# FoX heads half a head behind the GDN heads, two weight slots and a gather ring of six in a hybrid decoder step

## What is computed

```python
qkv_g, a_g, b_g, z_g, qkv_f, f_f, og_f = split_in(rmsnorm(hp, norm_mix[l]) @ w_in[l])
# GDN, 8 heads of 128: short causal conv + SiLU on q|k|v, gated delta rule in chunks,
#   output = rmsnorm_head(o) * silu(z)
# FoX, 8 heads of 128: softmax attention with query/key norm and forget gates,
#   output = rmsnorm_head(o) * sigmoid(og)
hp = hp + merge_heads(o_gdn, z_g, o_fox, og_f, ...)          # concat @ w_out
hp = hp + peer(rmsnorm(hp, norm_ffn[l]), w_query, sub_keys, expert_u, expert_v)
```

## Time and profile before

| what | us |
|---|---|
| median of three runs | 4675.52 |
| the profiled execution, its own time | 4657.51 |
| its span | 4655.7 |
| group a: norm; heads; output, norm and routing | 0 to 54; 54 to 907; 917 to 1212 |
| group b: norm; heads | 1212 to 1293; 1293 to 2414 |
| group b: output projection; norm; routing | 2427 to 2600; 2600 to 2655; 2655 to 2985 |
| rest of the experts | 2985 to 4656 |

### The profile page before, as it was taken

The page is one execution under the profiler, slowest core; times in us unless marked ns, Lnnn a source line. Parts: engine busy times, 40 slices in busy tenths (PEclk is TensorE's granted clock), DMA queues, the critical chain, the costliest instruction groups (busy, mean ns, idle before and its releaser), DMA issues. The chain is left out here.

```text
span 4655.7 us, 35143 instructions
## 1 busy us (share of the span) xinstructions
PE 2418.1 (52%) x11713; PEld 1909.2 (41%) x11713; DVE 3374.0 (72%) x4421; ACT 545.6 (12%) x1307; POOL 2361.1 (51%) x1217
## 2 busy tenths in 40 slices
PE   6999999898488888888759564200000000000000
PEld 5888888677466656666547443100000000000000
DVE  1333333307749989989877588799898989989998
ACT  1222222200122212222210010000000000000000
POOL 1110001000226676656565322288888888888886
PEclk8999999799699999999859777655555555555555
DMA  6666666386759999999999855499999999999998
GB/s 188 210 189 203 210 203 192 112 291 228 265 209 402 410 391 393 395 391 395 339 363 408 309 203 203 154 416 422 404 419 405 411 413 420 420 412 422 411 417 355
DMA packets 443932, 1513.69 MB, mean 325 GB/s; under 512 B 42044, under 2 KB 276208, under 8 KB 277848
## 3 DMA queue, kind: packets, MB, share of 16 engines
q0 software_dynamic: 161840, 1158.85, 61.7%
q1 hardware_dynamic: 269240, 251.94, 17.0%
q10 hardware_dynamic: 12672, 100.67, 5.4%
HBM read 1384.96 MB, written 126.21 MB: 325 GB/s over the span
## 5 line engine op out<-in xcount | busy, mean ns | idle before, releaser
L1929 DVE SCALAR_TENSOR_TENSOR ex_y<-ex_ring,ex_wt,ex_y 128x2048 f32<-128x2048 f32 x538 | 1264.4, 2350 | 122.5 <-DMA ex_ring<-in_peer_v_dram,idx_all 74.4
L1914 DVE CUSTOM_DVE_ANT_0 ex_ring<-ex_ring,ex_xi 128x2048 f32<-128x2048 f32 x544 | 1244.7, 2290 | 141.2 <-DMA ex_ring<-in_peer_u_dram,idx_all 50.5
L1836 POOL DMA_INDIRECT ex_ring<-in_peer_u_dram,idx_all x384 | 794.4, 2069 | 341.2 <-DVE ex_hid L1914 136.3
L1836 POOL DMA_INDIRECT ex_ring<-in_peer_v_dram,idx_all x384 | 823.5, 2145 | 221.7 <-DVE ex_hid L1914 115.9
L1868 PE MATMUL ex_fold<-ex_y,const 128*32 128x512 f32 (+1 forms) x48 | 24.9, 683 | 1113.4 <-DVE ex_y L1929 1043.5
L1836 POOL DMA_INDIRECT ex_ring<-in_peer_v_dram,ex_idx_s x160 | 316.3, 1977 | 316.2 <-DVE ex_hid L1914 144.6
L1868 PEld LDWEIGHTS ex_fold<-ex_y,const 128*32 128x32 f32 (+1 forms) x48 | 6.3, 136 | 1131.6 <-DVE ex_y L1929 1044.4
L1836 POOL DMA_INDIRECT ex_ring<-in_peer_u_dram,ex_idx_s x160 | 315.1, 1969 | 200.3 <-DVE ex_y L1929 139.7
L843 PE MATMUL heads_b_pj<-xnT_b,lead 128*128 128x304 f32 x1376 | 410.3, 436 | 5.1 <-PEq L270 3.7
L843 PE MATMUL heads_a_pj<-xnT_a,heads_a_w 128*128 128x256 f32 x1216 | 310.1, 393 | 1.7 <-DMA heads_a_w<-in_w_in_dram 1.7
L843 PEld LDWEIGHTS heads_b_pj<-xnT_b,lead 128*128 128x128 f32 x1376 | 255.6, 198 | 79.4 <-issue 15.0
(11 more groups left out here) (568 smaller groups left out, 4156.3 us busy)
## 6 DMA issues: line engine op xcount, KB each, us to landing
lead<-w_scratch SPq DMA_DIRECT2D x43, 1024.0 KB, 9.1
heads_a_w<-in_w_in_dram SPq DMA_DIRECT2D x38, 1024.0 KB, 6.1
w_scratch<-heads_a_w ACTq DMA_DIRECT2D x38, 1024.0 KB, 4.4
lead<-in_w_in_dram SPq DMA_DIRECT2D x26, 1024.0 KB, 5.7
w_scratch<-lead ACTq DMA_DIRECT2D x26, 1024.0 KB, 4.6
heads_b_w<-w_scratch SPq DMA_DIRECT2D x21, 1024.0 KB, 9.5
out_a_w<-in_w_out_dram SPq DMA_DIRECT2D x7, 2048.0 KB, 14.3
w_out_scratch<-out_a_w ACTq DMA_DIRECT2D x7, 2048.0 KB, 9.5
```

What stands on the lines that cost most here:

```text
L1836: pool.indirect_dma_start(self.ring[:, i % RING, :], None, self.tables[which], bass.IndirectOffsetOnAxis(ap=self.index(s, g, k), axis=0)). ...
L1914: nc.vector.tensor_tensor_reduce(ring, ring, self.tokens(s)[:], 1.0, 0.0, ALU.mult, ALU.add, self.hid[:, g % 2, k:k + 1]).then_inc(self.se ...
L1929: nc.vector.scalar_tensor_tensor(y, ring, wt, y, ALU.mult, ALU.add).then_inc(self.sem["consumed"], 1)
```

## The change

The gather ring gets a sixth place. In group b the heads have two weight slots, `lead` alone, and no buffer `w`. The segments are ordered q, k, v, z of GDN and then q, k, v, og of FoX, and segment j starts at mark 12.5 (j - 3). FoX's head h starts at mark 100 h + 50. The items of group b's heads are spread over marks 0 to 850. Apart from W, all of the marks apply to both groups.

```diff
-RING = 5
+RING = 6
...
-G_Q, G_K, G_V, F_Q, F_K, F_V, G_Z, F_OG = range(8)
-BASES = (0, C_K, C_V, C_FQ, C_FQ + HEADS * HD, C_FQ + 2 * HEADS * HD, C_Z, C_OG)
+G_Q, G_K, G_V, G_Z, F_Q, F_K, F_V, F_OG = range(8)
+BASES = (0, C_K, C_V, C_Z, C_FQ, C_FQ + HEADS * HD, C_FQ + 2 * HEADS * HD, C_OG)
...
 def segment_mark(j, step):
-    return 12.5 * (j - 6) + 12.5 * step / KT
+    return 12.5 * (j - 3) + 12.5 * step / KT
+
+def fox_mark(h):
+    return 100.0 * h + 50
...
-    W, PJ = (5, 3) if samples else (3, 2)
+    W, PJ = (5, 3) if samples else (2, 2)
...
-            "w": ([P, W - 2, KT, HD],),
+            **({"w": ([P, W - 2, KT, HD],)} if W > 2 else {}),
...
             def cached():
...
-                            yield 100.0 * (h - 1) + step + 0.5 * i
+                            yield fox_mark(h - 1) + step + 0.5 * i
...
             def fox():      # the same line on SP, PE, ACT, DVE and POOL
-                    at, n = 100.0 * h, h + 1
+                    at, n = fox_mark(h), h + 1
...
             def items():    # on DVE; item_mark on ACT likewise
-                    yield 100.0 * HEADS * (i + 0.5) / quota
+                    yield (100.0 * HEADS + 50) * (i + 0.5) / quota
```

More of the change, by code:

```diff
@@ L1067, in fox @@
                 for h in range(HEADS):
-                    at, n, qkv = 100.0 * h, h + 1, B.f_qkvT[:, h % 2]
+                    at, n, qkv = fox_mark(h), h + 1, B.f_qkvT[:, h % 2]
                     yield at + 2
@@ L1332, in item_mark @@
             def item_mark(i):
-                return 100.0 * HEADS * (i + 0.5) / quota
+                return (100.0 * HEADS + 50) * (i + 0.5) / quota
             act.wait_ge(sem["f_cleared"], 5)
```

## The result

The changed kernel takes 4591.38 us (median of four runs, 4588.94 to 4603.0) against 4674.64 for the kernel before (four runs, 4667.34 to 4675.54): a ratio of 0.983, 95% interval 0.9811 to 0.985, 83 us less. Repeated on another chip it was 4594.38 against 4685.59, ratio 0.9817 (0.9777 to 0.9857), 91 us less. The forecast was 4646, with 4612 as its lower end: the sign was right, the gain nearly three times too small.

A forecast was written before the change was run, and what follows sets the result against it. DMA was taken to bound most of the second group's heads and the later experts, PE the first group's heads. Terms -24.0, -3 and -2.5 gave 4628.0 from 4657.5, plus 18 to the median: 4646 us, range 4612 to 4682.

The forecast's parts named there:

- the ending of the first group: End of first group's heads, 47.3 us before: set at 52 with FoX alone last, +5 us (0 to +12).
- Second group, opening: -24.6: Start of second group's heads: three projected segments ahead in place of six, 27.4 us in place of 52.0.
- Items over 850 marks: -48.4, and +50 at the end: Second group's heads: 2.43 fewer items each, 6.05 us a head; 19.4 items return in FoX's lone half head.
- Two slots: +8, and four more slices: +3: Second group's heads: late slices cost 1 us a head (0 to 40 us in all); extra weight loads 0 to 10.
- The recorded estimate by the rule of turns: Weight loads beside gathers: queues taken in turn would give a slice 5 to 6 us, the slot term 0.
- a head that does not shorten: Second group's heads: PE and DVE hand-overs lose half of the 48.4 us, total 4670 us; chance 0.20.
- the second slot as the limit: PE's slice waits in second group's heads: three short segments wait 2.7 us each, total 4703 us; chance 0.13.
- The ring: -12: Second group's heads: sixth place gives 1.5 us a head (0 to 20 in all); separately 2.5 us at routing's end.
- The third rival: DMA's idling in second group's head fronts vanishes, 32 us, and first group's body idling, 11; 4615 us, chance 0.17.
- First group: -3: First group's heads: PE's work stays; page loads -8.2, ending +5, body -5, first half head +3, table loads +2.
- The page loads' waits of 8.2 us: End of first group's opening: PE's slice waits of 2.33 and 5.88 us go as page loads come later, -8.2.
- From the profile to the median: +18: Whole kernel: median 18 us above the profiled execution (0.4%), assumed the same after the change.

The follow-up runs named there:

- the pair of experiments: Changed kernel with a ring of five: two slots, 4616.43 us, against three slots as before, 4614.2 us.
- old marks: Kernel before with a ring of 6 and two slots, its order, marks and spreading unchanged: 4656.48 us, ratio 0.9944.
- old marks, items over 850: Kernel before with ring of 6 and two slots, plus the second group's items spread over 850 marks: 4657.14 us.

## Why the prediction was right and wrong

The forecast gained 29.5 us, the runs 83: 54 us were missing. Four of its steps failed, and each is named below: the sixth place after the heads, put at 2.5 us; PE's busy time in the first group, taken for work that stays; the ending of the first group, put at +5 us; and the difference between profile and median, carried over as if it were constant. By the means at the end of this section the missing 54 us lie in the second group's heads (17), the rest of the experts (13), the first group's idle time (11) and its clock (19), less 6 elsewhere.

**Second group, opening: -24.6.** Right: 52.0 to 27.6 us.

**Items over 850 marks: -48.4, and +50 at the end.** Right, and shown by itself between the kernels with and without it: the eight heads gave 50 us (4.8 in each of the five from the second on, 10 in the first, 19 in the seventh, -3 in the last), the stretch behind them took 47 back, and the stage is 1 us shorter. In the change the middle heads fell by 6.5, the ring's part included. FoX's lone half head fits beside its items: 50.8 us, 49.2 of them up to the last item. The whole stretch behind the last GDN head grew by 54.7 us, though, since the wait for the next stage behind it went from 13.0 to 16.9 us.

**Two slots: +8, and four more slices: +3.** The slots cost 4 us of the stage by the pair of experiments, within the 1095.8 to 1102.4 us over which four profiles with the new marks and ring spread, and 0.7 to 1.4 us of waits on PE. So the term was too large. The recorded estimate by the rule of turns is wrong too: a slice without gathers beside it took 4.8 us, twice that is 9.6 and not 5 to 6, and the measured 9.1 does not speak against the rule. Both rivals that needed more, a head that does not shorten (0.20) and the second slot as the limit (0.13), are out. The slices did not show.

**The ring: -12.** Right in the heads, 11 us from a ring of five to six. The step that failed, in size, is "Where DMA is at 1.00 a sixth place gives nothing", from which the forecast gave the ring 2.5 us after the heads. A share of 1.01, as in the earlier trace rows, stood beside 405 to 419 GB/s, and the rest of the experts gained 7 us in the profiles compared and 15 in the mean. The single gather that I let fit into the routing's end gained nothing: the wait there went from 23.5 to 25.4 us. Behind the second group's heads up to six gathers are under way now. They land until 2370 us, with DMA at 1.01 and hardly an engine at work, and the next stage begins 16.0 us after POOL's last issue, where it was 12.2 (12.2 to 14.0 in the five profiles with five places, 14.2 to 16.1 in the nine with six); what the last 6 us of that wait for is not shown:

```profile
2358.00:2370.00 12.00, 0.00 (x0) 0.00 (x0) 0.38 (x1) 0.00 (x0) 3.06 (x3) 0.50 1.01 421
```

Together the second group's heads gave 32 us in the profiles for a forecast of 24: opening 24, the eight heads 62 for a forecast of 49, the end -55 for -50. The third rival (0.17, 4615 us) comes nearest to the time, and has 13 of its 20 further us in these heads; its other half, the idling in the first group's body, did not go as it had it, 22.6 to 17.5 us.

**First group: -3.** With the clock in it this is the largest miss of a stage. Two of its steps failed.

| kernel | stage | PE busy | mean clock | rest |
|---|---|---|---|---|
| before | 863.2 | 817.6 | 0.93 | 45.6 |
| old marks | 870.3 | 827.2 | 0.92 | 43.1 |
| old marks, items over 850 | 890.4 | 846.0 | 0.90 | 44.4 |
| change | 841.3 | 810.2 | 0.94 | 31.1 |
| before, without narrow matmuls | 772.0 | 723.9 | 0.98 | 48.1 |
| change, without them | 757.3 | 725.5 | 0.98 | 31.8 |

"PE works 817.6 of 852.7 us; that work stays" took busy time for work. It contains the clock: the same instructions were 818 to 846 us of busy time under the old marks, 830 in the mean of three profiles, and 807 to 810 in all seven profiles with the new ones. The stage took 863.2 to 890.4 us under the old marks and 838.2 to 841.6 in those seven. The row had the clock at 0.95 with PE at 97%, and I did not ask what had lowered it in a stage where PE hardly rests.

The other part is what PE does not work, 45.6 to 31.1 us. The page loads' waits of 8.2 us did go, as forecast, and one of 2.8 us for `heads_a_hist` came; the rest of the body's idle time fell by 2 us, where I had put 5. ACT loads its tables 8 times more, as forecast; what that costs was not separated. And the ending, which I had put at +5, gained 8.5: from the last projection to the next stage it went from 57.8 to 49.3 us. POOL's timeline shows why, first in the kernel before, then in the change; the next stage's first load on SP stands behind each.

```profile
906.41 0.95 POOL L1646 DMA_DIRECT2D out_gdn_sample_dram<-heads_a_sout  x1 [9.78 <-DVE heads_a_sout L1506]
...
917.12 0.33 SPq L1979 DMA_DIRECT2D hres_a<-in_x_sample_dram  x1
```

```profile
886.16 0.95 POOL L1651 DMA_DIRECT2D out_gdn_sample_dram<-heads_a_sout  x1 [19.56 <-DVE heads_a_sout L1511]
...
894.07 0.48 DVE L1615 SCALAR_TENSOR_TENSOR mixT_a<-heads_a_F,vecs,heads_a_gz 128x256 f32<-128x256 f32 x1 [0.58 <-PE heads_a_F L1148]
...
896.86 0.33 SPq L1984 DMA_DIRECT2D hres_a<-in_x_sample_dram  x1
```

The stage ends 10.7 us after the store of GDN's last sample states is issued, in both. It does so in 13 of the 14 profiles, to 0.05 us (11.9 us in the one of the change without narrow matmuls), while the time from the last output to the next stage is 9.8 us in the five with the old marks and 2.3 to 3.5 in the others. No run leaves the store out. Before, nothing ran beside it. Now FoX's last half head does, up to 894.55 us, and is free. My working stopped at the last output and left the wait behind the store out.

**From the profile to the median: +18.** I carried the difference between the profiled execution and the median over unchanged. That was the fourth failed step, worth about 28 us, as much as all of the forecast gain. The profiles differ by things that the change reduces: the half-clock spells of the first group (7, 17 and 36 us more busy time than in the change, in three profiles of its old program) and, with a ring of five, the length of two stages (the second group's heads took 1134.2, 1139.0 and 1146.0 us in profiles with the old marks and ring, the rest of the experts 1622 to 1631). What makes these two stages vary was not looked into. Its profiled execution was a good one in each. By the means of these profiles the second group's heads gave some 41 us, the rest of the experts 15, the first group's idle time 14 and other stages took back 6, in all about 64; the pair without narrow matmuls is 70 us apart. The remaining 19 and 27 us of the 83 and 91 are then what the clock in the first group gave, by subtraction; the mean busy times there, 830 and 809 us, say 21. Why the new marks meet the shorter spells more steadily was not tested.

## What to carry to other kernels

Busy time is not work: where PE is the limit, read the granted clock of a middle stretch and, when it is under 1.00 without idle time, look for runs of matmuls with few columns; the same program then varies from run to run, and a forecast from one lucky profile misses what steadier code gains. A DMA share of 1.00 still leaves room when the bytes per second move, so price a deeper ring by those. And follow a stage to the first instruction of the next one: what is left behind the last result, a store or gathers that land, can cover a tail for nothing.

## What was not expected of the hardware

PE's clock fell to 0.50 with PE busy in every microsecond by the profile, in and between bursts of matmuls of 4 columns; with 28 of these 32 left out it stood at 1.00 for whole heads. Strewing them, with one projection matmul of 256 columns after about three, did not prevent it. Each microsecond at half clock cost about 0.5 (heads of 102.4 us with 10.2 us of spells, 105.8 with 17.1). The 16 DMA engines read 1.01 of busy share both at 405 and at 419 GB/s. And slices landed as slowly as before, 9.6 us in the median and 19.1 at most, in a stage that had only one segment between a load's issue and its use, and still PE waited for 1.4 us at most.
